# An expert loop with a ring of five weight slots and one buffer of gathered tokens

## What is computed

```python
def moe_ffn(x, router_w, router_bias, w1, w3, w2, sw1, sw3, sw2):
    shared = (jax.nn.silu(xf @ sw1) * (xf @ sw3)) @ sw2
    s = jax.nn.sigmoid(jnp.matmul(xf, router_w, preferred_element_type=jnp.float32))
    ...
    _, eidx = lax.top_k(jnp.where(emask, sb, NEG), TOP_K)
    sel = jnp.take_along_axis(s, eidx, axis=-1)
    gates = sel / jnp.sum(sel, axis=-1, keepdims=True) * ROUTED_SCALE
    routed = grouped_experts(xf, eidx, gates, w1, w3, w2)
    return (shared + routed).reshape(bsz, s_len, d)
...
    def step(out, args):
        tok, g, e = args
        xe = xpad[tok]
        h = jax.nn.silu(xe @ w1[e]) * (xe @ w3[e])
        y = (h @ w2[e]) * g[:, None].astype(xe.dtype)
        return out.at[tok].add(y), None
```

## Time and profile before

| | us |
|---|---|
| median of 3 runs | 1345.64 (1344.99 to 1346.11) |
| the profiled execution | 1344.79 |
| its span, first to last instruction | 1342.9 |
| TensorE busy | 1301.0 (97%) |
| VectorE, ScalarE, GpSimd busy | 475.1, 310.3, 81.2 |

### The profile page before, as it was taken

One profiled execution on the slowest core, in us unless ns is written; L12 is line 12 of the kernel. 1 busy time (PEld: TensorE's weight loads), 2 busy tenths in 40 slices (PEclk: granted clock), 3 DMA queues, 4 the chain that ended last, 5 costly groups with the idle time before them and its releaser, 6 DMA issues.

```text
span 1342.9 us, 23014 instructions
## 1 busy us (share of the span) xinstructions
PE 1301.0 (97%) x9694; PEld 746.3 (56%) x9694; DVE 475.1 (35%) x791; ACT 310.3 (23%) x747; POOL 81.2 (6%) x93
## 2 busy tenths in 40 slices
PE   9999999999999999998999999999999999999988
PEld 4555665555555455554488457555555555555544
DVE  1584533333332323333511246232333323233244
ACT  1244422121221221111210234222122221112112
POOL 2443100000000000000100021000000000000000
PEclk9999999999999999999999999999999999999999
DMA  9820689999999999999764537899999999999991
GB/s 306 308 96 32 251 304 415 420 420 421 421 421 420 421 420 420 421 421 394 246 234 145 197 112 277 323 410 421 419 420 421 421 420 421 421 421 421 420 383 76
DMA packets 83151, 462.00 MB, mean 344 GB/s; under 512 B 7024, under 2 KB 7504, under 8 KB 34672
## 3 DMA queue, kind: packets, MB, share of 16 engines
q1 hardware_dynamic: 81040, 454.15, 83.7%
q0 software_dynamic: 2016, 6.43, 1.6%
HBM read 459.50 MB, written 1.05 MB: 343 GB/s over the span
## 4 chain that ended last, share of the span: by engine, by line
PE 78%; DMA 18%; DVE 2%; issue 1%; ACT 0%; SPq 0%; DVEq 0%
PE ps L1269 27%; DMA ring<-in_exp_w_dram 17%; PE ps L1309 12%; PE ps L1331 4%; PE ps L918 4%; PE ps L1462 4%; PE ps L1208 4%; PE ps L1105 3%; PE ps L1023 3%; PE ps L1177 2%; PE ps L1129 2%; PE ps L1279 1%; PE ps L1169 1%; PE ps L1080 1%; PE ps L1441 1%
## 5 line engine op out<-in xcount | busy, mean ns | idle before, releaser
L1309 PE MATMUL ps<-ring,qkT 128*32 128x512 f32 x1984 | 232.9, 595 | 4.1 <-issue 2.8
L2186 DVE TENSOR_TENSOR o_tok<-ps,o_tok 128x1024 f32<-128x1024 f32 x124 | 150.6, 1222 | 156.4 <-PE ps L1331 156.4
L2191 DVE TENSOR_TENSOR y_lo<-ps,y_hi 128x1024 fp32r<-128x1024 f32 x62 | 75.9, 1224 | 213.6 <-ACT y_hi L1694 213.6
L1269 PE MATMUL ps<-ring,xT 128*64 128x256 f32 x1008 | 124.5, 385 | 14.7 <-DMA ring<-in_exp_w_dram 14.6
L1309 PEld LDWEIGHTS ps<-ring,qkT 128*32 128x32 f32 x1984 | 61.5, 109 | 128.8 <-issue 127.6
L1269 PE MATMUL ps<-ring,pT 128*64 128x256 f32 x992 | 124.3, 385 | 5.9 <-DMA ring<-in_exp_w_dram 5.8
L1669 ACT ACTIVATE roped<-ps 128x256 f32<-128x256 f32 x64 | 24.6, 384 | 454.6 <-PE ps L1269 454.6
L1269 PE MATMUL ps<-ring,proj 128*64 128x256 f32 x1008 | 121.8, 379 | 0.0
L1269 PE MATMUL ps<-ring,gb_row 128*64 128x256 f32 x992 | 121.5, 379 | 0.0
L2175 DVE SCALAR_TENSOR_TENSOR roped<-roped,rows,ps 128x256 f32<-128x256 f32 x64 | 30.7, 480 | 236.6 <-ACT roped L1669 236.6
L1269 PEld LDWEIGHTS ps<-ring,xT 128*64 128x64 f32 x1008 | 71.0, 136 | 73.6 <-issue 35.8
(11 more groups left out here) (308 smaller groups left out, 1464.3 us busy)
## 6 DMA issues: line engine op xcount, KB each, us to landing
ring<-in_exp_w_dram SPq DMA_DIRECT2D x158, 2048.0 KB, 22.8
ring<-in_exp_w_dram SPq DMA_DIRECT2D x54, 1024.0 KB, 8.8
ring<-in_od_w_in_dram SPq DMA_DIRECT2D x6, 2048.0 KB, 8.6
ring<-in_ple_w_gate_dram SPq DMA_DIRECT2D x4, 2048.0 KB, 15.4
ring<-in_ev_w_in_dram SPq DMA_DIRECT2D x3, 2048.0 KB, 20.0
ring<-in_ev_w_o_dram SPq DMA_DIRECT2D x2, 2048.0 KB, 10.4
x_tok<-in_exp_w_dram SPq DMA_DIRECT2D x4, 1024.0 KB, 7.6
ring<-in_exp_w_dram SPq DMA_DIRECT2D x8, 512.0 KB, 17.9
```

What stands on the lines that cost most here:

```text
L1269: ins = pe.matmul(ps[b * SLOTS:(b + 1) * SLOTS, 2, w * FE:(w + 1) * FE], xe(odd, c)[:, u * P + b * SLOTS:u * P + (b + 1) * SLOTS], views[b ...
L1309: ins = pe.matmul(ps[q:q + TILE_SLOTS, 4 + half, :], hT[:, f, h0:h0 + TILE_SLOTS], down_rows(b, f, half), start=(f == 0), stop=(f == 1))
L2186: dve.tensor_tensor(ys, ps[:, bank:bank + 2, :], ys, ALU.add).then_inc(sem("y_added"), 1)
L2191: dve.tensor_tensor(y_lo[:, :], ps[:, 4:6, :].rearrange("p b n -> p (b n)"), y_hi[:, :], ALU.subtract)\
```

## The change

- The ring has a fifth slot, `FIFTH`: the places in which expert 4 lay. Expert e goes to `HOMES[e % 5]`, so experts 4, 9, 14 ... 59 go there, their w2 in three pieces (one half in rows of 4 KiB, the other in two pieces with rows of 2 KiB). `pair_load` is written anew, with single transfers of 1 MiB; pair m's room goes to experts 5 + 2m and 6 + 2m. w3 and half of w2 of expert 4 are loaded beside the shared expert's weights, its w1 without waiting for `y_begin`.
- There is one buffer of gathered tokens, in `xT` and `pT` (w3 of the fifth slot needs the other's place). All four quarters of the next octet are gathered in an octet's last pair, where the tokens in the buffer are used up after the w3 matmuls: quarter 0 between the projections, 1 after the transposes, 2 between the down halves, 3 after them.
- The linear projection goes to bank 3. `silu` starts after the gate projection. In a pair without gathers the scatter halves stand before and after the transposes.
- The shared expert's down pieces are in pairs 24, 25, 26 and 28, the transposes of p in pair 28. `y_acc` is begun by GpSimd, from the two parts of x, after pair 0's gate projection.

```diff
-UNROLL = 4
-EARLY = 2 * RING
-AGAIN = EARLY + 2
-NEXT_EARLY = AGAIN + RING
+FIFTH = RING
+HOMES = (3, 0, 1, 2, FIFTH)
+SHARED_AT = (PAIRS - 8, PAIRS - 7, PAIRS - 6, PAIRS - 4)
...
+            def down_load(L, e, rows=(0, 1)):
+                w2, to = a["exp_w2"][L, e], home(e)
+                rows_f = w2.rearrange("(p f) n -> p f n", f=2)
+                if to < RING:
+                    sp.dma_start(ring[:, to, DOWN0:DOWN0 + 2 * D], w2.rearrange(rows_of, c=2)).then_inc(down_loaded[to], 16)
+                else:
+                    if 0 in rows:
+                        sp.dma_start(roped_flat[:, 2944:2944 + D], rows_f[:, 0, :]).then_inc(down_loaded[to], 16)
+                    if 1 in rows:
+                        for half in range(2):
+                            sp.dma_start(extra_w2[1][half], rows_f[:, 1, half * PIECE:(half + 1) * PIECE]).then_inc(down_loaded[to], 16)
...
+            def pair_load(L, m):
+                after = [e for e in range(5, NE) if room_of(e) // 2 == m]
+                whole = [e for e in after if e < NE - 2]
+                sp.wait_ge(sem("exp_gate"), L * PAIRS + m + 1)
+                for e in after:
+                    gate_load(L, e)
+                sp.wait_ge(sem("exp_up"), L * PAIRS + m + 1)
+                for e in whole:
+                    lin_load(L, e)
+                if NE - 1 in after:
+                    last_lin_load(L)
+                sp.wait_ge(sem("exp_down"), L * PAIRS + m + 1)
+                for e in whole:
+                    down_load(L, e)
+                if NE - 1 in after:
+                    last_down_load(L)
...
                     if k == e0 + 2:
                         shared_load(L)
+                        lin_load(L, 4)
+                        down_load(L, 4, (0,))
...
+                def pe_step(m, o, u, gather_next=True, selT_next=True, scatter_last=True):
                     par = u % 2
+                    gathers = gather_next and u == 3
...
+                    exp_up(m, o, u, 0)
+                    if gathers:
                         scatter(m - 1, 0, 1 - par)
...
+                    if m in SHARED_AT:
+                        shared_down(SHARED_AT.index(m))
+                    if gathers:
+                        gather(o + 1, 0)
+                    exp_up(m, o, u, 1)
+                    if gathers:
+                        scatter(m - 1, 1, 1 - par)
+                    elif scatter_last:
+                        scatter(m - 1, 0, 1 - par)
                     h_transpose(m)
                     if selT_next:
                         sel_transpose(m + 1, o + 1 if u == 3 else o, (u + 1) % 4)
+                    if scatter_last and not gathers:
+                        if m in SHARED_AT:
+                            pe.wait_ge(sem("shared_added"), 4 * L + SHARED_AT.index(m) + 1)
+                        scatter(m - 1, 1, 1 - par, bank=0)
+                    if gathers:
+                        pe.wait_ge(sem("xe_copied"), 4 * o + (4 * O0 + 5))
+                        gather(o + 1, 1)
+                    exp_down(m, 0, by_half=not selT_next)
+                    if gathers:
+                        pe.wait_ge(sem("xe_copied"), 4 * o + (4 * O0 + 6))
+                        gather(o + 1, 2)
+                    exp_down(m, 1, by_half=not selT_next)
+                    if gathers:
+                        pe.wait_ge(sem("xe_copied"), 4 * o + (4 * O0 + 7))
+                        gather(o + 1, 3)
...
-                    if j == 0 and later(o, 2):
-                        act.wait_ge(sem("exp_up"), 4 * o + (M0 - 4))
+                    if j == 0 and later(o, 1):
+                        act.wait_ge(sem("exp_up"), 4 * o + M0)
...
                 def silu(m):
-                    act.wait_ge(sem("exp_up"), m + (M0 + 1))
+                    act.wait_ge(sem("exp_gate"), m + (M0 + 1))
...
+                pool.wait_ge(sem("exp_gate"), L * PAIRS + 1)
+                for t in range(NT):
+                    step(pool.tensor_tensor(y_acc[:, t, :].rearrange("p (n c) -> p n c", c=DC),
+                                            x_hi[:, t, :].rearrange("p (c n) -> p n c", c=DC),
+                                            x_lo[:, t, :].rearrange("p (c n) -> p n c", c=DC), ALU.add))
+                    pool.tensor_scalar(y_acc[:, t, :], y_acc[:, t, :], ALPHA, None, ALU.mult).then_inc(sem("y_begun"), 1)
```

More of the change, by code:

```diff
@@ new lines, in ffn_load, with last_lin_load @@
+            def ffn_load(L, e):
+                gate_load(L, e)
+                lin_load(L, e)
+                down_load(L, e)
+            def last_lin_load(L):
+                s, e = home(NE - 2), NE - 2
+                for half in range(2):
+                    cols = slice(half * UP_N // 2, (half + 1) * UP_N // 2)
+                    sp.dma_start(ring[:, s:s + 2, UP_N + cols.start:UP_N + cols.stop],
+                                 a["exp_w3"][L, e:e + 2].rearrange("e (p c) f -> p e (c f)", c=DC)[:, :, cols])\
+                      .then_inc(w_loaded[s + half], 16)
@@ new lines, in last_down_load @@
+            def last_down_load(L):
+                s, e = home(NE - 2), NE - 2
+                for half in range(2):
+                    cols = slice(half * PIECE, (half + 1) * PIECE)
+                    for b in range(2):
+                        w2 = ring[:, s + b, DOWN0:DOWN0 + 2 * D].rearrange("p (c f) -> p c f", c=2)
+                        sp.dma_start(w2[:, :, cols], a["exp_w2"][L, e + b].rearrange("(p c) f -> p c f", c=2)[:, :, cols])\
+                          .then_inc(down_loaded[s + half], 16)
@@ L565, in _ @@
+                    if k == e0 + RING:
+                        fifth_load(L)
+                        for m in range(PAIRS - 2):
+                            pair_load(L, m)
                         k = e0 + NE
@@ L2252, in _ @@
                 for u in range(1, 4):
[L2253 removed]
+                    dve_step(u, 0, u)
                 with dve.Fori(1, OCTETS - 2) as o:
```

434 lines of the change are left out of this document (153 added, 281 removed).

## The result

| | kernel before | kernel after |
|---|---|---|
| median, us | 1345.57 (1344.40 to 1346.65, 6 runs) | 1350.88 (1348.83 to 1351.17, 6 runs) |
| profiled execution, us | 1344.79 | 1348.83 |
| its span, us | 1342.9 | 1346.7 |
| first expert loop, us | 458.06 | 460.24 |
| second expert loop, us | 457.28 | 460.11 |

The account below looks back on a forecast made before the run. It took the expert loops to be fed by DMA at 421 GB/s. Terms of +4.8 us in layer 0 and +5.5 in layer 1, together +10.3 on the profiled 1344.79, gave 1355 us, range 1347 to 1364.

Parts of the forecast that it names:

- The order of the last transfers: Loop's end: w3 of expert 61 lands at T - 15.9, so the loop ends 4.1 us a layer later.
- T: Landing of the last byte in layer 0, put at 633.7; loop end T + 1.9 before, T + 6.0 after.
- w3 of expert 61 to the end: Pair 30's second up weights landing to loop end: 21.9 us, with TensorE already waiting 2.5 us early or more.
- One buffer of gathered tokens: nothing: Four gather quarters moved into each octet's last pair: same 55 us per octet against 59.8 of data, no cost.
- The 16.4: Time in us taken for the one late pair with four gather quarters, in 88 us of work from pair 24.
- The refill after pair 0: Two w2 loads instead of one follow pair 0's down projection, closing the rate sag: -1.6 and -0.85 us.
- The fifth slot's w2: Eleven experts' w2 in short rows, 10% slower, 0.25 us each, less the old kernel's 0.44: +2.3 us a layer.
- 1 MiB in place of 2 MiB transfers: Expert loads in the loops: smaller queued transfers still run at 421 GB/s, no cost; bounds +5 and -4 us a layer.
- silu and the gate product lie under scatter and up matmuls: Activations in each pair: silu after the gate, gate product after both projections, both covered, no cost.
- y_acc on GpSimd: Four operations after pair 0's gate, done by 193 us at the latest, first add near 197: no cost.
- the tail's order is covered: Rival: w3 of expert 61 is not what TensorE waits for, the 4.1 us go: 1345 to 1348, chance 0.15.
- The bunched gathers make TensorE the bound: Rival: gather quarters wait by more than 4.6 us per octet, 28 us over two layers: 1373, chance 0.06.

Follow-up runs that it names:

- b_order: Kernel before, with only w1 of experts 62 and 63 issued ahead of w3 of 60 and 61: 1357.73 us, ratio 1.0094 to the kernel before.
- a_both: Kernel after, with the last load groups paired as before and the shared expert's pieces in pairs 5, 6, 9, 10: 1344.02 us, 0.9995 of the kernel before.
- a_order: Kernel after, with only the last load groups paired again as in the kernel before: 1347.84 us, ratio 1.0026 to the kernel before.
- a_refill: Kernel after, with expert 6's w2 load issued behind pair 1's gate loads, so one w2 follows pair 0's down projection: 1352.06 us, 1.0051 of the kernel before.
- b_d8: Kernel before, with expert 8's w2 issued by itself right behind pair 0's down projection: 1343.56 us, ratio 0.9986 to the kernel before.
- a_rows: Kernel after, with the fifth slot's 4 KiB-row w2 half loaded in two pieces of 2 KiB rows: 1350.86 us, ratio 1.0044 to the kernel before.
- a_merge: Kernel after, with two 1 MiB transfers made one of 2 MiB in three load groups of five: 1354.89 us, ratio 1.0077 to the kernel before.
- a_silu: Kernel after, with silu again waiting for both projections of a pair: 1358.16 us, ratio 1.0100 to the kernel before.
- b_bunch: Kernel before, with all four gather quarters of an octet in its last pair, from octet 1 on: 1385.21 us, ratio 1.0299 to the kernel before.
- a_piece: a_both with the fourth shared piece back in pair 26: 1343.61 us, ratio 0.9991 to the kernel before.
- a_less: Kernel after, loading the fifth slot's second w2 half (2 KiB rows) for expert 4 alone, output not the reference's: 1326.32 us, 0.9859 of the kernel before.

## Why the prediction was right in sign, and where its steps failed

The forecast was 1355, +10.3 us over the profiled execution; measured are +3.8 us between the profiled executions and +4.8 by the ratio. The range and the sign held; the size was forecast at more than twice what it is. Step by step, with the completion records of the DMA engines (the trace holds when each of the 16 engines finished its part of a transfer; what follows is worked out from them and from the timeline):

```
last expert transfer of a loop      before           after
first loop:  mean of 16 engines     630.8            629.5
             slowest engine         633.0            630.9
             end of the loop        635.6            637.4
second loop: mean of 16 engines     1295.4           1296.8
             slowest engine         1297.3           1298.1
             end of the loop        1299.8           1304.45
```

- **The order of the last transfers, +4.1 a layer: right, and not the only holder.** From the slowest engine's landing to the end were 2.6 and 2.5 us before and are 6.5 and 6.3 after: +3.9 and +3.8. T was forecast at 633.7 and was 633.0. w3 of expert 61 to the end: 21.6 us, forecast 21.9. b_order shows the 4.1 us alone. That TensorE was waiting at all when w3 of 61 landed, on which the term rests, held by 0.45 us where the prediction saw 2.5 us or more: there it was lucky.
- **"One buffer of gathered tokens: nothing": the step that failed, at no cost to the number.** The prediction let TensorE be fed by data at pair 24's gate and found it 2.5 us early or more at w3 of expert 61. But pair 23 before it is a bunched pair as well: 17.48 us against 14.95 of data, so pair 24 begins 2.5 us late. And the six pairs 24 to 29 took 611.64 - 521.97 = 89.7 us, not the 88.2 of the prediction's terms, as a bunched pair takes 17.48 and not 16.4. That is 4.0 us, and the margin was gone but for the 0.45 us. The 16.4 was a slip that its own rows show: four pairs of 13.79 less three of 12.7 leave 17.1.

  A second thing it left out is the order of transfers in the loop's middle. Pair 23's gate waits for w1 of expert 47, which now stands in the load group with expert 48, and starts 327.3 us into the loop where it started at 324.6 before; with the bunched quarters, pair 24 begins at 344.8 against 339.6. From there to pair 30 TensorE needs about as long as before (89.7 us against 90.2, of which 0.6 is a wait for data). a_both against a_order (1.4 and 2.4 us a loop) shows what TensorE's late work costs once the last transfers no longer hide it; it moves the shared pieces and not the gathers, so that the gathers and pair 23's late start are the cause rests on these pair times. Had the order been left as it was, the prediction would have called the change nearly free and been wrong by these 1 to 2 us a layer.
- **The refill after pair 0, -1.6 and -0.85: about right.** In the completion records 7 MiB are there 1.7 and 1.0 us earlier in the loop than before, 13 MiB 1.8 and 1.1. a_refill takes back 0.6 and 0.9 us of it; b_d8's gain can't be counted for it, as its data comes only 0.0 to 0.2 us earlier at the end.
- **The fifth slot's w2, +2.3 a layer: mis-sized.** Between the first 7 MiB and the mean landing of the last transfer the kernel after lost 0.85 and 0.6 us, with everything in it. Its short rows alone, by the 100 MiB in the middle of the loop, cost 1.5 us a layer (last section), where the prediction had 2.7 before it took off the 0.44 of the old kernel's own short rows. The rates of 2 us windows and of the tail, from which I took 10%, hold more than the row length; I take it to be the slow last engines of a queue that ends and the edges of the window, which no run here separates. a_rows bounds one half of it at 0.5 to 1 us a layer. This is the largest part of the overshoot, some 3 us in all.
- **A term that wasn't there: the spread of the 16 engines.** In the kernel before the slowest engine was 2.3 and 1.9 us behind the mean at the last expert transfer, after it 1.4 and 1.3. That gives back 0.9 and 0.6 us a layer. I have no experiment for why the spread is smaller. It differs between executions too: at w3 of expert 61 the slowest engine of a_refill was 3.2 us behind the mean in one loop and 5.05 in the other.
- **1 MiB in place of 2 MiB transfers, nothing: right.** 418 to 420 GB/s over whole stretches, and a_merge took 250.8 us for the same 100 MiB. The Trainium skill (DMA: Bandwidth & Descriptors, section Measured) has 78% of peak for a transfer of 1 MB, measured on transfers issued by GpSimd; in SyncE's queue here, which is never empty in the loop, the trace disagrees with it as a price for each transfer. What the coarser grain did cost in a_merge, 2.7 us a loop, was no matter of bandwidth.
- **silu and the gate product lie under scatter and up matmuls: right for the kernel as changed**, where the transposes never wait after pair 0, but it names what covers them only by the way. a_silu (+7.3 us) and b_bunch (+40 us) show that this cover is what the change stands on.
- **y_acc on GpSimd: covered, with less to spare.** The first two of its four operations, and the first add on VectorE that waits for them:

```profile
182.60 3.73 POOL L687 TENSOR_TENSOR o_tok<-x_hi,x_lo 128x1024 f32<-128x1024 f32 x1 [7.80 <-issue]
186.42 2.84 POOL L690 TENSOR_SCALAR o_tok<-o_tok 128x1024 f32<-128x1024 f32 x1
...
197.52 2.55 DVE L2142 TENSOR_TENSOR o_tok<-ps,o_tok 128x1024 f32<-128x1024 f32 x2
```

  The fourth ends at 195.9 us, not by 193, 1.6 us ahead of the add: the additions took 3.7 us each and not the 2.87 of the earlier trace rows.

The sum as measured: -1.7 (refill) + 0.85 (short rows and all else in the loop) - 0.9 (spread) + 3.9 (tail) = +2.2 in the first loop, -1.0 + 0.6 - 0.6 + 3.8 = +2.8 in the second, as in the table of the loops. The forecast had 4.8 and 5.5; the other 1.2 us between forecast and traces lie outside the loops.

Of the rivals, "the tail's order is covered" was nearest to what is left out of the sum: TensorE's own work stood 0.45 us from covering it. "The bunched gathers make TensorE the bound" had its mechanism in the wrong place. The quarters don't wait for their copies; it is the pairs without a quarter that lose their cover, and the change had put another there.

## What to carry to other kernels

Where a loop is fed by DMA and ends in a stretch of TensorE's unbroken work, look for the last wait for data, not for the sum of waits: everything behind it counts in full, and here a wait of 0.45 us at its far end meant two causes at once, so that undoing either one alone showed little (0.0 to 0.8 us of 2.2 and 3.1). Work moved out of a pair leaves a hole where it stood: before you move it, ask which other engine's result was being made beside it. Work that can be placed freely belongs in the last long wait; in a_piece it cost nothing there and kept the clock up.

## What the runs showed of the hardware

- **A long wait can cost more than itself.** In the first loop of the kernel after, TensorE waited 2.87 us, until 434.63, and its granted clock was 0.5 (1.2 GHz in place of 2.4) for 3.4 us. In the other kernels' loops all waits of 2.46 to 2.66 us and the 6.17 us of b_order had such a stretch too, and those of up to 2.14 us had none. But neither had the waits of 3.13 and 3.04 us in a_merge's second loop, while in a_silu's second loop two waits of 1.07 and 0.50 us, 1.2 us apart, were followed by one. So the length of a single wait doesn't decide it. The row and the window:

```profile
434.63 3.31 PE L1231 MATMUL ps<-ring,xT 128*64 128x256 f32 x16 [2.87 <-DMA ring<-in_exp_w_dram]
```

```profile
434.00:438.00 4.00, 3.37 (x20) 0.57 1.01 420
```

  Ahead of the last wait for data it cost nothing (the second loop of the kernel after had no such stretch and is as long); in the tail (b_order, a_both) it did.
- **The 16 DMA engines drift apart in a queue that never empties.** By the completion records, the first and the last engine's part of one transfer to the ring landed 2.6 us apart at 200 us, 3.5 at 300, 5.1 at 420 and 7.5 at 590 in the kernel before (after: 1.9, 1.8, 3.4, 6.5). A transfer has landed only when its slowest part has, so TensorE sees the slowest engine, while the GB/s show the mean. The distance grows in steps of 0.6 to 1.6 us. A 16 KiB packet of the instruction queue keeps one engine for 1.05 us (there are 79 of them); that these packets are the cause was not tried.
- **Short rows behind a full queue are cheap.** In the loops of the kernel after the mean packet of SyncE's queue took 314 ns for 8192 B, 162 for 4096 B and 86 for 2048 B, that is 2 x 162 / 314 = 1.03 and 4 x 86 / 314 = 1.10 times the time of the same bytes in 8 KiB packets. For the fifth slot's w2 this gives an estimate of (0.03 + 0.10) x 1.25 x 11 = 1.8 us a layer. The landings say 1.5: from the 50th to the 150th MiB of a loop, in which 6.7 of these experts lie, the kernel before took 250.1 and 249.9 us, the kernel after 251.0 and 250.8, 0.93 us more in both, 0.14 an expert. The experiments stand where they should: 250.2 in both loops of a_less, which leaves out the 2 KiB rows, and 251.4 and 251.3 in a_rows, which has nothing but them.
